# Gate factor taken into the heads' product, chunk columns read in place, and side work moved in a hybrid decoder layer

## The reference

```python
proj = jnp.einsum('btd,dp->btp', xn, w_in)
gb, gc, hc, zc, q, k, v, o, zm, ig, fg = jnp.split(proj, ...)
yc, conv_new = short_conv(gc * hc, conv_buf, conv_w)
y_conv = gb * yc * jax.nn.silu(zc)
# one chunk of a head:
s = jnp.einsum('bhjd,bhsd->bhjs', q, k) * d
num = jnp.einsum('bhjs,bhsv->bhjv', s, v) + inter[..., None] * jnp.einsum('bhjd,bhdv->bhjv', q, c_prev)
den = jnp.sum(s, axis=-1) + inter * jnp.einsum('bhjd,bhd->bhj', q, n_prev)
h = num / jnp.maximum(jnp.abs(den), jnp.exp(-m_t))[..., None]
c_new = decay[..., None, None] * c_prev + jnp.einsum('bhs,bhsd,bhsv->bhdv', w_last, k, v)
# after all chunks:
h = h * lax.rsqrt(jnp.mean(h * h, axis=-1, keepdims=True) + EPS)
h = h.transpose(0, 2, 1, 3).reshape(B, T, M_WIDTH) * mh_norm_gain
y_m = (h * jax.nn.sigmoid(o)) * jax.nn.silu(zm)
out = jnp.einsum('btw,wd->btd', jnp.concatenate([y_conv, y_m], axis=-1), w_out)
```

## Time and profile before

| what | value |
|---|---|
| median of 3 runs | 1103.79 us (1103.05 to 1104.08) |
| profiled execution | 1105.74 us, its span 1103.7 us |
| PE busy | 1027.2 us (93%), 9052 matmuls |
| DVE busy | 657.3 us (60%), 1156 instructions |
| POOL busy | 440.8 us (40%), 477 |
| ACT busy | 423.4 us (38%), 868 |
| mean granted TensorE clock | 0.979 |
| chain that ended last | PE 61%, DVE 22%, ACT 5%, POOL 4%, issue 3%, DMA 3% |

### The profile page before, as it was taken

One profiled execution on the slowest core, in us unless ns is written; L12 is line 12 of the kernel. 1 busy time (PEld: TensorE's weight loads), 2 busy tenths in 40 slices (PEclk: granted clock), 3 DMA queues, 4 the chain that ended last, 5 costly groups with the idle time before them and its releaser, 6 DMA issues.

```text
span 1103.7 us, 22725 instructions
## 1 busy us (share of the span) xinstructions
PE 1027.2 (93%) x9052; PEld 776.4 (70%) x9052; DVE 657.3 (60%) x1156; ACT 423.4 (38%) x868; POOL 440.8 (40%) x477
## 2 busy tenths in 40 slices
PE   3799799999889988999999999999999999999995
PEld 2555545455478777999889899989889999444442
DVE  6786756664667776556775546567755544434343
ACT  6555443423334343334543443436343432211111
POOL 5211355445454484623542341427042330542422
PEclk9999899999889999999999999999999999999998
DMA  9686642924561256591605272943253659465651
GB/s 246 175 190 138 160 111 63 236 66 143 198 207 53 84 165 215 162 322 62 223 21 189 93 248 65 314 143 124 68 181 106 220 140 344 140 216 210 232 207 76
DMA packets 192077, 180.86 MB, mean 164 GB/s; under 512 B 44600, under 2 KB 152260, under 8 KB 191972
## 3 DMA queue, kind: packets, MB, share of 16 engines
q1 hardware_dynamic: 160880, 142.76, 41.8%
q0 software_dynamic: 7600, 25.03, 6.2%
q10 hardware_dynamic: 23492, 11.63, 3.6%
HBM read 120.48 MB, written 50.19 MB: 155 GB/s over the span
## 4 chain that ended last, share of the span: by engine, by line
PE 61%; DVE 22%; ACT 5%; POOL 4%; issue 3%; DMA 3%; SPq 1%; DVEq 0%; ACTq 0%; POOLq 0%
PE bank L1337 10%; PE bank L1339 10%; PE bank L1338 10%; PE bank L1562 4%; PE bank L1563 4%; PE bank L1561 4%; DVE xs L207 3%; DVE Wl L207 2%; DVE yc L207 2%; DVE gatebuf L207 2%; PE bank L1138 1%; PE bank L1140 1%; PE bank L1139 1%; PE bank L1494 1%; PE bank L1495 1%
## 5 line engine op out<-in xcount | busy, mean ns | idle before, releaser
L1337 PE MATMUL bank<-xTh,Wh 128*128 128x256 f16 x768 | 211.6, 275 | 12.8 <-ACT bank L207 8.1
L1338 PE MATMUL bank<-xTl,Wh 128*128 128x256 f16 x768 | 211.4, 275 | 0.0
L1339 PE MATMUL bank<-xTh,Wl 128*128 128x256 f16 x768 | 211.4, 275 | 0.0
L1138 PE MATMUL bank<-xTh,Wh 128*128 128x512 f16 (+2 forms) x440 | 122.8, 313 | 3.2 <-ACT tom L207 1.0
L1139 PE MATMUL bank<-xTl,Wh 128*128 128x512 f16 (+2 forms) x440 | 123.1, 312 | 0.0
L1140 PE MATMUL bank<-xTh,Wl 128*128 128x512 f16 (+2 forms) x440 | 123.1, 312 | 0.0
L1337 PEld LDWEIGHTS bank<-xTh,Wh 128*128 128x128 f16 x768 | 75.9, 99 | 25.8 <-ACT bank L207 6.9
L1338 PEld LDWEIGHTS bank<-xTl,Wh 128*128 128x128 f16 x768 | 75.9, 99 | 10.9 <-issue 0.7
L1339 PEld LDWEIGHTS bank<-xTh,Wl 128*128 128x128 f16 x768 | 75.9, 99 | 9.5
L1337 PE MATMUL bank<-xTh,xs 128*128 128x256 f16 x288 | 78.8, 274 | 2.0 <-DVE xs L207 2.0
L1339 PE MATMUL bank<-xTh,xs 128*128 128x256 f16 x288 | 78.9, 274 | 0.0
(11 more groups left out here) (529 smaller groups left out, 2857.1 us busy)
## 6 DMA issues: line engine op xcount, KB each, us to landing
xTh<-x_ops SPq DMA_DIRECT2D x12, 1280.0 KB, 8.9
xTl<-x_ops SPq DMA_DIRECT2D x12, 1280.0 KB, 12.2
wst<-in_w_in SPq DMA_DIRECT2D x25, 512.0 KB, 5.0
xs<-in_x_prompt SPq DMA_DIRECT2D x22, 512.0 KB, 4.0
y_ops<-ysumst POOLq DMA_DIRECT2D x16, 512.0 KB, 3.2
xTh<-x_ops SPq DMA_DIRECT2D x12, 512.0 KB, 5.0
xTl<-x_ops SPq DMA_DIRECT2D x12, 512.0 KB, 5.7
out<-xs POOLq DMA_DIRECT2D x11, 512.0 KB, 2.9
```

Of the source, the lines that this page charges most:

```text
L1138: mm(out, wh[:, k, :], xh, start=(k == 0), stop=False)
L1337: mm(out, wh[:, k, :], xh, start=(first and k == 0), stop=False, skip_group_check=not first)
L1338: mm(out, wh[:, k, :], xl, start=False, stop=False, skip_group_check=not first)
L1339: last = mm(out, wl[:, k, :], xh, start=False, stop=(k == KT // 2 - 1), skip_group_check=not first)
```

## The change

- `mhg` is scaled by 0.25/WS once in the prologue. `(to + 1)` moves into the product with `zs` (`gate_product`), `mhg` into the product with the heads (`heads_out`), and the instruction on `to` goes. The same for `tom`.
- `sel` and its copy go; the readers take the columns out of `cols` (`col`, `col_of_chunks`). PE waits for `sel_ready` in block 0 alone, and in head 0 for a new `parts_ready`.
- `den` is made by four instructions that read the bank, in place of two copies, an absolute value and a max.
- In streamed heads `factors` comes behind `seed` and `head_scaled`.
- In head 0: in block 0 the x parts of V move into Q, and those of Q to its end, on ACT and DVE; on DVE the x parts come behind `at_end`, where they came before it; those of HC in block 1 (units 14 and 15) go to O; those of O go between the norm's steps. The gates' scan of blocks 1 and 2 moves from GB to ZC, their turn to O. In ZM, `zs` comes first, then the mixed part, then G.
- Token sums: POOL's units of head 0 move earlier in the blocks, ACT's and DVE's with them; those of block 2 of head 0 and block 1 of head 1 are spread otherwise.
- The splits for head 1: the sums' split of the first pair is made before V's; ACT makes four at the end of ZC; DVE two at ZC, two between the norm's steps, one at ZM.

```diff
 T0_PRO = 0
 T1_PRO = 4
-X_SQUARE = [{V: 6, Q: 7, GC: 8, HC: 9, ZC: 10, O: 11}, {K: 12, V: 13, Q: 14, HC: 15}, {K: 16}]
-X_PARTS = [{V: 5, Q: 6, GC: 7, HC: 8, ZC: 9, O: 10}, {K: 11, V: 12, Q: 13, HC: 14}, {K: 15, V: 16}]
+X_SQUARE = [{V: 6, Q: 7, GC: 8, HC: 9, ZC: 10, O: 11}, {K: 12, V: 13, Q: 14, O: 15}, {K: 16}]
...
 RAW_ORDER = [K, Q, V, GC, HC, GB, ZC, O, ZM]
 RAW_SLOT = {K: 0, Q: 1, V: 2, GC: 3, HC: 4, GB: 2, ZC: 0, O: 1, ZM: 3}
 RAW_SECOND = (GB, ZC, O, ZM)
 SPLITS = 17
-FIRST_SPLIT, HALF_SPLIT = [0, 3, 9, 11], [1, 4, 10, 12]
-V_SPLIT = 2
-T_SPLIT = [5, 7, 13, 15]
+FIRST_SPLIT = [[], [0, 5, 9, 11], [0, 3, 9, 11], [0, 3, 9, 11]]
+HALF_SPLIT = [[], [1, 6, 10, 12], [1, 4, 10, 12], [1, 4, 10, 12]]
+V_SPLIT = [None, 4, 2, 2]
+T_SPLIT = [[], [2, 7, 13, 15], [5, 7, 13, 15], [5, 7, 13, 15]]

...
@@ -1004,22 +1013,21 @@
                     pool.wait_ge(mx_states, g + 1)
                     dst = c_s[:, bass.ds(g, 1), :, :].rearrange("b h d v -> d (b h) v")
                     pool.dma_start(dst, cs[:, :, 0:P]).then_inc(cs_out, 16)
-                    x_power(15)
-                    token_sums(0)
...
                 if b == 0:
                     x_power(11)
                     store_mixed(g, 1)
-                if b in (1, 2):
-                    token_sums((2, 5)[b - 1])
+                if b == 1:
+                    x_power(15)
+                    token_sums(2)
                 if b == NB - 1:
                     pool.wait_ge(s_free, nth(g, b) * 3 + 3)
                     pool.dma_start(c_p[0, bass.ds(g, 1), :, :].rearrange("h d v -> d (h v)"), cn[:, 0:P]).then_inc(cn_out, 16)
...
-                for u in ((), (10,), (14,))[B] if B < 3 else ():
-                    token_sums(u)
+                if B == 2:
+                    token_sums(14)
                 pool.wait_ge(t0_free, s_t0(nth(g, b), "hT") + 1)
                 y_operands(*before)
                 store_y(*before, 1)
-                if B == 2:
-                    token_sums(15)
+                if B in (1, 2):
+                    token_sums((10, 15)[B - 1])
                 if b == 0:
...

-                    pe.wait_ge(sel_ready, n + 1)
+                    if b == 0:
+                        pe.wait_ge(sel_ready, g + 1)
+                    pe.wait_ge(parts_ready, b + 1)
                     pe.wait_ge(a_free, n * 3)
                     m = mparts[:, tok0(b):tok0(b) + BT]
                     if n:
...
-                        for i in {GC: (0, 1), GB: (2,), ZC: (3, 4), O: (5, 6)}.get(t, ()):
+                        for i in {GC: (0, 1), ZC: (2, 3, 4, 5), O: (6,)}.get(t, ()):
...
+                mark(tt(mparts[64:64 + H, block_of], rest, mparts[32:GR, block_of], ALU.subtract).then_inc(parts_ready, 1), parts_ready, b + 1)
...
-                    did(ts(tom[:, :], tom[:, :], 1.0, mhg[:, bass.ds(g, 1)], ALU.add, ALU.mult))
                     dve.wait_ge(mx_tanh, 2 * g + 2)
                     mark(stt(zsm[:, :], tzm[:, :], 1.0, src, ALU.add, ALU.mult).then_inc(t0_free, 1), t0_free, at + 1)
                     dve.wait_ge(t0_free, at + 1)
-                    mark(stt(Gm[:, :], tom[:, :], 0.25 / WS, zsm[:, :], ALU.mult, ALU.mult).then_inc(mx_g, 1), mx_g, g + 1)
...
+                before = (n - 1) // NB
                 dve.wait_ge(t0_full, at + 1)
                 dve.wait_ge(g_done, n)
-                mark(tt(dp[:, :], src[:, :], G[:, :], ALU.mult).then_inc(t0_free, 1), t0_free, at + 1)
+                mark(stt(dp[:, :], src[:, :], mhg[:, before:before + 1], G[:, :], ALU.mult, ALU.mult).then_inc(t0_free, 1), t0_free, at + 1)
...
-                    j, before = evacuations(g, b, O)
-                    dve.wait_ge(p_free[j], before + 1)
-                    did(ts(to[:, :], to[:, :], 1.0, mhg[:, bass.ds(g, 1)], ALU.add, ALU.mult))
                     dve.wait_ge(tanh_done, 2 * n + 2)
                     mark(stt(zs[:, :], tz[:, :], 1.0, src, ALU.add, ALU.mult).then_inc(free, 1), free, left + 1)
                     dve.wait_ge(free, left + 1)
-                    mark(stt(G[:, :], to[:, :], 0.25 / WS, zs[:, :], ALU.mult, ALU.mult).then_inc(g_done, 1), g_done, n + 1)
+
+            def gate_product(g, b):
+
+                n = nth(g, b)
+                j, before = evacuations(g, b, O)
+                dve.wait_ge(p_free[j], before + 1)
+                mark(stt(G[:, :], to[:, :], 1.0, zs[:, :], ALU.add, ALU.mult).then_inc(g_done, 1), g_done, n + 1)
...
-                mark(pick(sel[:, :, :], cols[:, 1 + CH * b:1 + CH * (b + 1), :, bass.ds(g, 1)].rearrange("p c k o -> p c (k o)"))
-                     .then_inc(sel_ready, 1), sel_ready, n + 1)
...
-                    mark(reciprocal(rec[:, :], den[:, :]).then_inc(rec_ready, 1), rec_ready, n + 1)
-                    dve.wait_ge(h_sq, n + 1)
...
-                        last = tt(eh[:, 2 * P * i:2 * P * (i + 1)].rearrange("p (c v) -> p c v", c=2), nv,
-                                  wide(hf[:, 2 * i:2 * i + 2], P), ALU.mult)
-                    mark(last.then_inc(n_free, 1), n_free, n + 1)
+                    head_norms(n)
+                    if first and O in X_PARTS[b]:
+                        x_low_part(X_PARTS[b][O])
+                    if b in S_LOW_NORMS:
+                        token_sums_low(S_LOW_NORMS[b])
+                    if b == NB - 1:
+                        split_low(1, 4)
+                    head_means(n)
+                    if first and O in X_SQUARE[b]:
+                        x_gain(X_SQUARE[b][O])
+                    if b == NB - 1:
+                        split_low(1, 5)
+                    head_scaled(n)
                 if b == 0:
...
+                    two = den[:, 2 * i:2 * i + 2]
+                    sums = N[i][:, 0:2 * DV1].rearrange("p (c v) -> p c v", c=2)[:, :, P]
+                    did(stt(two, sums, 1.0, col_of_chunks(g, b, 0, 2 * i, 2 * i + 2), ALU.mult, ALU.max))
+                    did(stt(two, sums, -1.0, two, ALU.mult, ALU.max))
                 mark(reciprocal(rec[:, :], den[:, :]).then_inc(rec_ready, 1), rec_ready, n + 1)

...
-                if b == 0:
-                    dve.wait_ge(prod, product_at(g, b, 0, M1))
-                if n == NB:
-                    dve.wait_ge(dp_ready, n)
-                if b == 0:
-                    factors(g)
                 if B:
                     head_means(n - 1)
-                mark(pick(sel[:, :, :], cols[:, 1 + CH * b:1 + CH * (b + 1), :, bass.ds(g, 1)].rearrange("p c k o -> p c (k o)"))
-                     .then_inc(sel_ready, 1), sel_ready, n + 1)
                 seed(g, b, 0)
                 if B:
                     head_scaled(n - 1)
+                if b == 0:
+                    factors(g)
                 second_of_second(g, b, 0, qf[:, HALF:BT], True)
                 if b == 1:
                     dve.wait_ge(t1_full, s_t1(g, "hT") + 1)
-                    mark(tt(ymm[:, :], T1[:, 0:MIX], Gm[:, :], ALU.mult).then_inc(t1_free, 1), t1_free, s_t1(g, "hT") + 1)
+                    mark(stt(ymm[:, :], T1[:, 0:MIX], mhg[:, g:g + 1], Gm[:, :], ALU.mult, ALU.mult).then_inc(t1_free, 1), t1_free, s_t1(g, "hT") + 1)
                 heads_out(g, b, s_t0(n, "hT"), A)
...
                         mixed_start(g, b, t, first)
                     at_half(g, b, t, first)
                     if first:
                         gate_chain(b, t)
+                        if b == 0 and t == Q:
+                            x_parts(b, V)
                     if b == 0 and t == HC:
                         mixed_conv(g)
                         did(copy(u[:, 0:2], um[:, META:META + 2]))
                     evacuate(g, b, t)
-                    if first:
-                        if t in X_PARTS[b]:
-                            x_low_part(X_PARTS[b][t])
-                        if t in X_SQUARE[b]:
-                            x_gain(X_SQUARE[b][t])
+                    if t == ZM:
+                        if b == 0:
+                            mixed_start(g, b, t, first)
+                        gate_product(g, b)
                     at_end(g, b, t, first)
+                    if first and t != O and (b or t != V):
+                        x_parts(b, t)
                     if t in S_LOW[b]:
                         token_sums_low(S_LOW[b][t])
                     if b == NB - 1:
                         if t == GC:
                             split_low(1, 0)
                             split_low(1, 1)
-                        if t == GB:
+                        if t == ZC:
                             split_low(1, 2)
-                        if t == ZC:
                             split_low(1, 3)
-                            split_low(1, 4)
-                        if t == O:
-                            split_low(1, 5)
+                        if t == ZM:
                             split_low(1, 6)

             GATE_COUNTS = [1, 3] + [t1(0, b, "gates", True) for b in range(NB - 1)]
@@ -2852,6 +2865,7 @@
             x_gain(0)
             dve.wait_ge(t1_full, 1)
```

(1 more changed line is left out.)

197 lines of the change are left out of this document (100 added, 97 removed).

## The result

The changed kernel's median is 1097.70 us (1096.54 to 1098.91) against 1103.93 us of the kernel before on the same chip: the recorded ratio is 0.9938, 95% interval 0.9918 to 0.9958 (the quotient of these two medians, 0.9944, lies inside it). It is 6.2 us faster by the medians and 6.8 by the ratio, clear of the noise. Forecast were 37.8 us, 1066.0. The sign was right and the size was wrong by a factor of six; 1097.70 lies above the range of 1057 to 1087.

A forecast was written before the change was run, and what follows sets the result against it. PE, busy 93%, bounds the kernel; only its idle and low-clock time, 62.1 us in eight windows, can be won. Window gains 2.5 + 8.0 + 2.0 + 1.6 + 7.5 + 8.0 + 5.5 + 2.7 = 37.8 us give 1066.0, range 1057 to 1087.

The forecast's parts named there:

- The factors, "they move behind it: 2.7": Starts of heads 2 and 3 (510 to 945 us): six small instructions move behind the seed, 2.7 us won.
- Rival B: Head 0: POOL's moved token sums slow DVE's x parts and splits beside them; gain only 20 us, 1084; chance 13%.
- Window 47 to 100, "2.5": Head 0: the wait of 3.75 goes but three smaller ones come; 2.5 of 8.1 us won, bounds 0 and 8.1.
- Window 100 to 145, "I charge 2.7 here: 8.0": Head 0: waits of 2.85 and 2.83 go with their clock, less 2.7 for a grown wait; 8.0 of 12.9 us won.
- Rival A: Blocks 0 and 1 of head 0: DVE's backlog travels to the next wait; gain only 28 us, 1076; chance 17%.
- Window 145 to 188, "2.0": Head 0: the wait of 3.71 for `cn` behind the gates' scans goes with its clock, less 3.4; 2.0 us won.
- Windows 248 to 302 and 302 to 317, "7.5" and "8.0": Waits behind splits, a token part and `to` go with their clock: 7.5 of 8.6 and 8.0 of 9.7 us won.
- 372 to 440, "5.5": Head 1: the seed's wait of 2.24 goes with 1.8 of clock, plus 1.5 from small waits; 5.5 of 10.7 us won.
- Gate factor: 16 instructions on `to` go; gain on PE's path at two places, 115.29 (wait of 2.85) and 310.09; products cost nothing.
- The clock: PE's clock falls behind long waits: one of about 3 us costs some 5 to 6, one of 1.3 costs itself.
- purse of 62 us: PE's idle time plus low-clock loss in eight windows between 47 and 945 us, together 62.1 us, which the change could win.
- rival D: All waits of the windows go but those of the first: gain 45 us, 1058; chance 6%.

The follow-up runs named there:

- e1_factors_late: The changed kernel with the six factor instructions of a head moved behind the heads' product: 1087.62 us, ratio 0.9837 to the kernel before.
- e3_pool_waits: The changed kernel with one added wait, so POOL begins the second pair's weight sums only when the factors are written: 1089.41 us, ratio 0.9859.
- e4_token0_back: The changed kernel with POOL's token sum of unit 0 back from tile Q of block 1 to behind the sample states: 1098.23 us, ratio 0.9922.
- e5_x_pair_late: The changed kernel with DVE's second pair of x parts at the end of GC of block 1 instead of Q: 1092.94 us, ratio 0.9884.
- e10_scan_gb: The changed kernel with factors late, token sum 0 back, x pair late, parts 9 and 10 moved, gates' scan back in GB: 1080.53 us, ratio 0.9771.
- e12_store11: The changed kernel with factors late, token sum 0 back, x pair late, parts 9 and 10 moved, store of part 11 early: 1079.22 us, ratio 0.9742.

## Why the prediction was wrong

*The factors, "they move behind it: 2.7".* This is the step that failed most. The seed's wait did go (536.50 to 519.37, 2 us more won at the heads turned of head 2), and 6.6 us were lost at once behind it; the window gave −7.8. I had named what stood ahead of the factors and not what stood behind them: the read of the second product, for which PE waits too, in a bank of its own. The cost of the new place was put at nothing. And I priced the six at their duration in the old place, 1.7 us; they took 5.5 beside POOL's sums. e1_factors_late prices the place at 11.2 us, e3_pool_waits says that 8.7 of these are POOL's hold. With the factors late, the two heads give 2.7 us by start times, as forecast. (The six took 1.5 before, not "up to 1.7".)

*Rival B* had the mechanism, "POOL's sums only change their victims", and looked in the wrong place for it. Most of it came from the weight sums, which the change does not move, and struck six instructions that the change moved under them; the sign that I wrote down ("x parts, splits or G of over 2 us") did not name these. But that sign showed too: in block 1 two gains took 2.96 and 2.95 us and PE waited behind both. The token sum beside the first cost 1.8 us or less than can be told (e4_token0_back); the y sum beside the second was not taken away by itself.

*Window 47 to 100, "2.5"*, gave 0.1. The wait of 3.75 went, and small ones of 0.5 to 1.9 us, six of them, came. DVE is busy 42.8 of the 53 us, and moving work within this block won nothing, which is near the lower bound that I had given.

*Window 100 to 145, "I charge 2.7 here: 8.0".* The two waits went as forecast; PE begins the argument matmul of block 1 at 126.42, 9.2 us earlier than before. Two things ate it. The first pair, moved behind `mparts`, was put at nothing there; ACT's part waits 6.04 us for its gain, ahead of `qf` and the exps, and PE waits 1.05 and 2.54 behind them. Of that the token sum beside it explains 1.05 and 0.4 (e4_token0_back); that the other 2.12 are ACT's part ahead of the exps is read from the rows and not tested. The second pair, ahead of the scores' product, was seen, and mis-sized: 2.6 us of queue, when it took 4.2, its gain at 2.95 beside POOL, and PE's wait went from 1.27 to 4.91, with low clock behind. e5_x_pair_late got 6.0 us back by moving that pair. Rival A's sign, one wait of 3 to 5 us released by `cs` between 130 and 180, is there; but it is one place and one reason, not a backlog that travels: after the move the next state's wait grew by 0.6 us and the one in block 3 by 0.3.

*Window 145 to 188, "2.0".* The scan costs wherever it stands: 3.71 before, 2.56 now, 3.98 in GB again, 2.15 late in block 1 and 6.21 late in block 2, where POOL's sums nearly doubled the scan. Moving it to ZC was worth nothing (e10_scan_gb), and a gain of the whole 3.71 with its clock was wrong: the wait moved to the next `cn`.

*Windows 248 to 302 and 302 to 317, "7.5" and "8.0"* were right in size (7.0 and 8.6), and wrong in part in the cause: I gave the larger part to the splits, and undoing them costs 2.8 (± 3.4) in all. Several things stood ahead of the same waits, and putting one of them back costs little while the others stay away.

*372 to 440, "5.5".* The first wait went as said (2.24 to 1.04, with the clock), 2.8 us. I added "a quarter" of the small waits on no row, while the change put a part that waits for POOL ahead of the seed (3.04) and a store later than the load that waits for it (2.67). A third new wait, 1.99 for `eh` at 424.98, no run takes away by itself. I had read that ACT's parts "move" and not asked what each waits for.

*Gate factor.* Priced at two places, inside the windows' sums; alone it is 7.6 us, won in seven places of 0.3 to 3.3 us, since `to` stood ahead of `zs` or of G in every block.

*The clock.* As the prediction took it, windows with waits of 2.5 us and more have a granted clock below 1 (0.91 in 100 to 145, 0.97 in 372 to 440), and 188 to 302, with waits of 0.85 and 1.28, has 1.00. In smaller windows of the changed kernel the size of the wait does not decide alone: 80 to 90 has 0.83 behind a wait of 1.86, and 414 to 434 has 1.00 behind waits of 2.67 and 1.99. The purse of 62 us is not contradicted: e12_store11 takes 28.5 of it.

*The signs and the sums.* The clock in 302 to 317 (1.00), the seeds of heads 2 and 3 without a wait and the 39 instructions fewer came as written; "no PE wait over 2 us from 100 to 320" did not (2.54, 4.91, 2.56), and the sign of "wrong altogether", a loss of over 45 us left in these windows, did (52). Two of the numbers do not follow from their own terms: rival D's "All waits of these windows go but those of the first" is 62.1 − 8.1 = 54 by the purse and not 45, and the lower end of the forecast's bounds, 1058, comes out at 1054 with the windows that give the upper end of 1076.

The method behind it was a replay of queues with the durations of the old places. It found the gains and missed the costs: each gain was a wait with a row, each cost needed a row that the old trace could not have.

## What to carry to other kernels

When an instruction is moved in a queue, price it by what runs beside the new place, and name the next wait on each engine behind it: the move of six small instructions by two places cost 11.2 us over three heads. The gains of several things that stand ahead of the same waits do not add: the gate's factor alone won 7.6 us and `den` alone 2.1, and with the late factors they won 8.1 together; test each part on its own before adding. Side work in idle gaps is safe only if it waits for nobody and if no POOL sum runs beside it: a part that itself waits for POOL, put ahead of a seed, handed that wait to PE (3.04 us), and the scan, put beside a token sum, took 3.69 us for 1.22.

## What the runs showed of the hardware

A DVE instruction whose inputs lie in SBUF does not run slower beside POOL in proportion to its size; it is held until POOL's instruction is done. Four of the six ends at the start of head 2 lie within 0.1 us behind an end of POOL's (rows above), and with POOL held back the same six take 1.5 us. It struck instructions with one input from SBUF (`selm`, 80 x 2) as well as those with two, and large ones: the gain of 1.23 us began at 127.39, POOL's instruction ended at 129.28, and the gain ended at 130.35. Those with a bank among their inputs kept their time (0.16 us for `den` within a sum).

Counted over the 17 traces, for DVE instructions that start well within a TENSOR_TENSOR of POOL's (from 0.15 us behind its start to 0.5 before its end): none of 689 with a bank among the inputs took over 0.1 us more than its own shortest. All TENSOR_TENSORs, casts, copies and scans with SBUF inputs (377) did, as did 171 of 222 SCALAR_TENSOR_TENSORs (the other 51 are one instruction that is never seen alone), and they ended behind POOL's end by their own length less some 0.14 us. So the price is what is left of POOL's instruction, whatever the size of DVE's. Two forms with one SBUF input were not held: 7 RECIPROCALs of 128x4 (0.18 us each) and 19 TENSOR_SCALARs of 128x1 (0.15). Which of the two engines must begin first cannot be read safely: `dselm`, 0.02 us ahead of POOL's record, kept its 0.17, while `den` in the kernel before, 0.43 us ahead of it, was held to POOL's end.

The Trainium skill (GPSIMD Engine Reference, Key points) says that POOL shares its SBUF interfaces with VectorE and contends with DVE instructions that have two SBUF inputs or run in a 2-port mode. The traces agree for two inputs (the TENSOR_TENSORs above); whether the casts, the copies and `selm` ran in such a mode no run here shows.

The start of the program varies by 2.6 us among kernels that are alike there (the columns of block 0 at 46.6 to 49.2), behind waits for loads; a difference in the first 50 us of one trace is no effect.
